# Mixture of experts in fp32: the experts' output is weighted, gated and added onto the residual in memory instead of in a combine stage

## The reference, cut to what matters

```python
h2 = rms_norm(x, norm2_w[l]) * (1 + sc2) + sh2
x = x + g2 * moe_ffn(h2, ...)
# in moe_ffn, for each expert e and its rows xe:
gu = xe @ w_gate_up[e] + b_gate_up[e]
gate, up = jnp.split(gu, 2, axis=-1)
gate = jnp.minimum(gate, SWIGLU_LIMIT)
up = jnp.clip(up, -SWIGLU_LIMIT, SWIGLU_LIMIT)
act = gate * jax.nn.sigmoid(SWIGLU_ALPHA * gate) * (up + 1)
yb = act @ w_down[e] + b_down[e]
# after all experts
y_rows = yb.reshape(n_rows, d) * row_w[:, None]
return jnp.zeros_like(hf).at[row_tok].add(y_rows)
```

## Time and profile before

| | |
|---|---|
| median of 3 runs | 2898.56 us (2898.47 to 2901.44) |
| the profiled execution's own time | 2901.38 us |
| its span | 2899.8 us |
| TensorE busy | 2509.1 us, 87% |
| VectorE busy | 1846.0 us, 64% |
| ScalarE busy | 1428.9 us, 49% |
| GpSimd busy | 483.5 us, 17% |
| DMA over the span | 572.65 MB, mean 197 GB/s |

### The profile page before, as it was taken

How to read it: one execution, slowest core, us unless ns; L and a number is a source line. 1 busy time by engine, 2 the same in 40 slices (tenths; PEclk the granted TensorE clock), 3 DMA queues, 4 the chain that set the end, 5 groups by cost and what they waited for, 6 DMA issues and landing times. The chain is left out here.

```text
span 2899.8 us, 39631 instructions
## 1 busy us (share of the span) xinstructions
PE 2509.1 (87%) x11553; PEld 1953.5 (67%) x11554; DVE 1846.0 (64%) x2784; ACT 1428.9 (49%) x2282; POOL 483.5 (17%) x504
## 2 busy tenths in 40 slices
PE   5899959898957999999988999999899999899930
PEld 2688835555845777777766777778667778677720
...
DMA packets 420768, 572.65 MB, mean 197 GB/s; under 512 B 20722, under 2 KB 319218, under 8 KB 419698
## 3 DMA queue, kind: packets, MB, share of 16 engines
...
HBM read 526.93 MB, written 45.12 MB: 197 GB/s over the span
## 5 line engine op out<-in xcount | busy, mean ns | idle before, releaser
L1550 ACT ACTIVATE d_whi<-d_raw 128x1024 fp32r<-128x1024 f32 x528 | 532.3, 1049 | 245.1 <-PE psum L1750 216.1
L1746 PE MATMUL psum<-d_whi,d_xthi 128*128 128x512 f32 x1536 | 616.9, 402 | 30.8 <-DVE d_xtlo L1622 23.3
L1631 DVE TENSOR_TENSOR d_wlo<-d_raw,d_whi 128x1024 fp32r<-128x1024 f32 x462 | 550.8, 1218 | 87.1 <-ACT d_whi L1550 85.7
L1746 PE MATMUL psum<-d_whi,d_xtlo 128*128 128x512 f32 x1536 | 604.8, 394 | 0.0
L1746 PE MATMUL psum<-d_wlo,d_xthi 128*128 128x512 f32 x1536 | 603.0, 393 | 0.0
L1631 DVE TENSOR_TENSOR d_wlo<-slab,d_whi 128x1024 fp32r<-128x1024 f32 x268 | 358.0, 1367 | 119.1 <-ACT d_whi L1550 119.1
L1550 ACT ACTIVATE d_whi<-slab 128x1024 fp32r<-128x1024 f32 x268 | 271.9, 1052 | 188.8 <-PE psum L1750 188.8
L1746 PEld LDWEIGHTS psum<-d_whi,d_xthi 128*128 128x128 f32 x1536 | 289.2, 188 | 108.0 <-issue 35.2
L1746 PE MATMUL psum<-d_whi,d_athi 128*128 128x512 f32 x768 | 310.6, 404 | 25.7 <-DVE d_atlo L1637 25.7
L1746 PEld LDWEIGHTS psum<-d_whi,d_xtlo 128*128 128x128 f32 x1536 | 289.0, 188 | 63.6
L1746 PEld LDWEIGHTS psum<-d_wlo,d_xthi 128*128 128x128 f32 x1536 | 289.6, 189 | 58.4
...
## 6 DMA issues: line engine op xcount, KB each, us to landing
...
d_raw<-in_w_down_dram SPq DMA_DIRECT2D x66, 2048.0 KB, 7.7
b_raw<-in_w_ada_dram SPq DMA_DIRECT2D x8, 2048.0 KB, 8.4
e_y<-y_d SPq DMA_DIRECT2D x8, 2048.0 KB, 13.6
...
a_xin<-in_x_dram ACTq DMA_DIRECT2D x2, 2048.0 KB, 9.3
```

What stands on the lines that cost most here:

```text
L1550: nc.scalar.activation(whi[j % 2][:, part, :], raw[j % NRAW][:, part, :], ACT.Copy).then_inc(whi_ok, 1)
L1631: nc.vector.tensor_tensor(wlo[j % 2][:, part, :], raw[j % NRAW][:, part, :], whi[j % 2][:, part, :].bitcast(F32), ALU.subtract).then_inc(w ...
L1746: nc.tensor.matmul(to, m_[b][:, k, :], w_[w][:, k, :], start=(k == 0 and q == 0), stop=False)
```

## The change

- `y_d` and `combine_block` are gone. `x1_d` becomes `acc_d`, with 128 rows of padding more. The experts' scatter writes there with `compute_op=ALU.add`, by token instead of by token and choice.
- `output` moves from ScalarE to VectorE and multiplies PSUM by the row's weight and by `gate2`. In slab 5 it stands after `xt_low` and before pieces 2 and 3.
- The row's weight comes from `topw_d`, a copy of `topw_all` in memory that SP stores at the end of the mixer stage. GpSimd gathers 128 of them for each block, one 4-byte element per row, when it has copied the destinations, and waits for them. For that the entries of the list have a third number, the index of the weight: one VectorE copy more per tile and choice. Padding has weight 0.
- GpSimd splits no weights any more; VectorE splits all four pieces of all slabs, and SP's loads and TensorE wait for VectorE alone.
- Before the first group GpSimd clears the padding of `acc_d` and `topw_d` and waits for that.
- After the last scatter SP copies the 4 MB of `acc_d` to `out` in one transfer.

The diff, cut to its core (declarations of semaphores, `c_entry`'s width, the new argument of `expert_block` and TensorE's simpler wait for `wlo` are left out; of `combine_block` only the removal of its head is shown):

```diff
...
     s.extk_d = dram("extk_d", [s.H, 4, s.T], F32)
-    s.x1_d = dram("x1_d", [s.T, s.D], F32)
+    s.acc_d = dram("acc_d", [s.T + P, s.D], F32)
+    s.topw_d = dram("topw_d", [s.T * s.TOPK + P, 1], F32)
...
-    s.list_d = dram("list_d", [s.E * s.T, 2], I32)
-    s.y_d = dram("y_d", [s.T * s.TOPK + P, s.D], F32)
+    s.list_d = dram("list_d", [s.E * s.T, 3], I32)
...
         chanmean = sb("a_chanmean", [P, P], F32)
-        nolist = sb("a_nolist", [P, s.E * T // P, 2], I32)
+        nolist = sb("a_nolist", [P, s.E * T // P, 3], I32)
...
                 own.link(nc.gpsimd.memset(chanmean[:, :], 1.0 / DC))
-                own.link(nc.gpsimd.memset(nolist[:, :, 0:1], 0))
-                own.link(nc.gpsimd.iota(nolist[:, :, 1:2].rearrange("p (a n) c -> p a (n c)", n=P),
-                                        pattern=[[0, s.E * T // P // P], [1, P]], base=s.TOPK * T, channel_multiplier=0))
+                own.link(nc.gpsimd.memset(nolist[:, :, :], 0))
+                for c, base in ((1, T), (2, s.TOPK * T)):
+                    own.link(nc.gpsimd.iota(nolist[:, :, c:c + 1].rearrange("p (a n) c -> p a (n c)", n=P),
+                                            pattern=[[0, s.E * T // P // P], [1, P]], base=base,
+                                            channel_multiplier=0))
...
                                  ).then_inc(slab_in, 16)
+                sp.wait_ge(topw_ok, 1)
+                sp.dma_start(s.topw_d[0:T * K4, :].rearrange("(t p r) a -> p t (r a)", p=P, r=K4),
+                             s.topw_all[:, :, :]).then_inc(topw_st, 16)
+                sp.wait_ge(topw_st, 16)
...
                     act.wait_ge(x1_ok, i + 1)
-                    act.dma_start(s.x1_d[bass.ds(i * P, P), :], xt[b][:, :]).then_inc(x1_st[b], 16)
+                    act.dma_start(s.acc_d[bass.ds(i * P, P), :], xt[b][:, :]).then_inc(x1_st[b], 16)
...
                         nc.vector.tensor_copy(entry[b][r][:, 0:1], tokf[:, bass.ds(i, 1)])
-                        ins = nc.vector.tensor_scalar(entry[b][r][:, 1:2], tokf[:, bass.ds(i, 1)], float(K4), float(r),
+                        nc.vector.tensor_copy(entry[b][r][:, 1:2], tokf[:, bass.ds(i, 1)])
+                        ins = nc.vector.tensor_scalar(entry[b][r][:, 2:3], tokf[:, bass.ds(i, 1)], float(K4), float(r),
...
                                                  .broadcast_to([P, NT, K4]), ALU.mult))
+                dve.sem_inc(topw_ok, 1)
...
         xg = [sb(f"d_xg{b}", [P, D], F32) for b in range(2)]
-        entry = [sb(f"d_entry{b}", [P, 2], I32) for b in range(2)]
+        entry = [sb(f"d_entry{b}", [P, 3], I32) for b in range(2)]
+        roww = [sb(f"d_roww{b}", [P, 1], F32) for b in range(2)]
+        roww_in, pad_st, added, out_st = ([sem(f"d_roww_in{b}") for b in range(2)], sem("d_pad_st"),
+                                          sem("d_added"), sem("d_out_st"))
...
-        POOL_SLABS, HALF = (2,), NP // 2
-        own_pieces = [HALF if j in POOL_SLABS else NP for j in range(SLABS)]
-        PER_DVE, PER_POOL = sum(own_pieces), HALF * len(POOL_SLABS)
...
-            return PER_DVE * (g + 1) + sum(own_pieces[:j]) + pieces
-        def split_by_pool(g, j, pieces):
-            return PER_POOL * (g + 1) + HALF * POOL_SLABS.index(j) + pieces
+            return NP * (SLABS * (g + 1) + j) + pieces
...
                     gb, jb = (g, j - NRAW) if j >= NRAW else (g - 1, j - NRAW + SLABS)
-                    sp.wait_ge(wlo_ok, split_by_dve(gb, jb, own_pieces[jb]))
-                    if jb in POOL_SLABS:
-                        sp.wait_ge(wlp_ok, split_by_pool(gb, jb, HALF))
+                    sp.wait_ge(wlo_ok, split_by_dve(gb, jb, NP))
...
-                sp.sem_inc(wlo_ok, PER_DVE)
-                sp.sem_inc(wlp_ok, PER_POOL)
+                sp.sem_inc(wlo_ok, NP * SLABS)
...
                 load(0, total(sp), 0)
+                sp.wait_ge(added, 1)
+                sp.dma_start(out[0, :, :], s.acc_d[0:T, :]).then_inc(out_st, 16)
+                sp.wait_ge(out_st, 16)
...
                 for b in range(2):
-                    own.link(nc.gpsimd.iota(ydst[b][:, :], pattern=[[0, 1]], base=s.TOPK * T, channel_multiplier=1))
+                    own.link(nc.gpsimd.iota(ydst[b][:, :], pattern=[[0, 1]], base=T, channel_multiplier=1))
...
                 own.link(nc.gpsimd.memset(two[:, :], 0))
+                pool.dma_start(s.acc_d[T:T + P, :], yst[0][:, :]).then_inc(pad_st, 16)
+                pool.dma_start(s.topw_d[T * s.TOPK:, :], yst[0][:, 0:1]).then_inc(pad_st, 16)
+                pool.wait_ge(pad_st, 32)
...
                     def scatter(b):
-                        pool.indirect_dma_start(out=s.y_d[:, :],
+                        pool.indirect_dma_start(out=s.acc_d[:, :],
                                                 out_offset=bass.IndirectOffsetOnAxis(ap=ydst[b][:, :], axis=0),
-                                                in_=yst[b][:, :], in_offset=None).then_inc(y_st[b], 16)
+                                                in_=yst[b][:, :], in_offset=None, compute_op=ALU.add
+                                                ).then_inc(y_st[b], 16)
...
                         s.settle(pool)
+                        pool.indirect_dma_start(out=roww[b][:, :], out_offset=None, in_=s.topw_d[:, :],
+                                                in_offset=bass.IndirectOffsetOnAxis(ap=entry[b][:, 2:3], axis=0)
+                                                ).then_inc(roww_in[b], 16)
...
                         pool.wait_ge(xg_in[b], 16 * (g + 1))
+                        pool.wait_ge(roww_in[b], 16 * (g + 1))
...
                         s.settle(pool)
-                    for j in POOL_SLABS:
-                        for q in range(HALF, NP):
-                            part = slice(PIECE * q, PIECE * (q + 1))
-                            pool.wait_ge(whi_ok, NP * (SLABS * g + j) + q + 1)
-                            nc.gpsimd.tensor_tensor(wlo[j % 2][:, part, :], raw[j % NRAW][:, part, :],
-                                                    whi[j % 2][:, part, :].bitcast(F32), ALU.subtract).then_inc(wlp_ok, 1)
...
                 s.settle(pool)
+                pool.sem_inc(added, 1)
...
-                def output(g, jd, b, sh):
-                    act.wait_ge(dn_mm, CRED + 2 * DN * g + 2 * jd + (b + 1) * sh)
-                    act.wait_ge(y_st[b], 16 * (g + 1))
-                    nc.scalar.activation(yst[b][:, jd * SL:(jd + 1) * SL], psum[:, 2 * ((GU + jd) % 2) + b, :],
-                                         ACT.Copy).then_inc(y_ok, sh)
...
                                 turned(g, j - 1, b, sh)
-                            elif j > GU:
-                                output(g, j - 1 - GU, b, sh)
                         split(g, j + 1, [3] if j < GU else [2, 3])
-                    for b in range(blocks):
-                        output(g, DN - 1, b, sh)
...
+                def output(g, jd, b, sh):
+                    dve.wait_ge(dn_mm, CRED + 2 * DN * g + 2 * jd + (b + 1) * sh)
+                    dve.wait_ge(y_st[b], 16 * (g + 1))
+                    dve.wait_ge(roww_in[b], 16 * (g + 1))
+                    cols = slice(jd * SL, (jd + 1) * SL)
+                    nc.vector.scalar_tensor_tensor(yst[b][:, cols], psum[:, 2 * ((GU + jd) % 2) + b, :],
+                                                   roww[b][:, 0:1], s.gate2[:, cols], ALU.mult,
+                                                   ALU.mult).then_inc(y_ok, sh)
...
                                 turned(g, j - 1, b, sh)
+                            elif j > GU:
+                                output(g, j - 1 - GU, b, sh)
                         split(g, j + 1, [3] if j < GU else [2, 3])
+                    for b in range(blocks):
+                        output(g, DN - 1, b, sh)
...
-def combine_block(nc, s, a, out):
...
-        s.release(nc)
-        combine_block(nc, s, arrays, out)
...
```

71 lines of the change are left out of this document (6 added, 65 removed).

## The result

The changed kernel takes **2849.49 us** (median of 4 runs, 2844.66 to 2853.01), the kernel before 2900.0 us beside it (2898.47 to 2903.51): a ratio of 0.9823, 95% interval 0.9804 to 0.9842. So 50.5 us are gained where I forecast 106.6, and the time lies 4.5 us above the range's upper end of 2845. The sign was right, the size was not.

A forecast was written before the change was run, and what follows sets the result against it. Bounds: TensorE in two-block groups, VectorE pacing one-block groups, a serial combine at the end. Tail -90.8, loop -21.1, head and mixer +5.3 make -106.6 on 2901.4; set against the runs' median, 2792 us, range 2768 to 2845.

The forecast's parts named there:

- Tail: From the last scatter's start to the end: 26.2 us instead of 117.0, so 90.8 us less.
- D: Time the addition in memory adds to a scatter's landing: taken as 2 us, between 0 and 6.1.
- My estimate of 23.4 us: Final copy, if reads and writes both count against 358 GB/s; 17 us was taken, this would end some 6 us later.
- Head and mixer: Before the first group: padding clearing 4.3 us, casts 1, top-weights store nothing; together 5.3 us more.
- Two-block groups: Expert loop: TensorE's waits for xtlo go as outputs leave ScalarE, 10.7 us less in 6 groups, 5.8 in 8.
- One-block groups, VectorE: Expert loop: stalls beside GpSimd's split go, two pieces and two outputs come; 1.2 us less per group.
- the ring: Loop dependency through scatter, row weights, entry, gather and transposes: period 41.1 to 41.7 us plus D, 43.4 with D = 2.
- 41.7 if nothing else binds: One-block group's time in us by VectorE's work alone, instead of 42.9.
- One-block groups, GpSimd's chain: Scatter to row gather grows 6.8 us plus D, using up 8.0 of slack; 10 groups lose 0.5 us each.
- 1.1 us of slack: One-block groups: ScalarE begins to need the gathered rows 1.1 us after TensorE, counted within 8.0 us of slack.
- a lead of 3 us: After a two-block group the scatter leaves about 3 us earlier relative to TensorE's end, so 8 groups keep 1.2 us gain.
- rival (b): The scatter's addition is dear, D about 5, slowing one-block groups and the tail: 2833 us; chance 24%.

The follow-up runs named there:

- this part alone: The kernel before with VectorE splitting every weight piece and GpSimd none, nothing else changed: 2882.66 us, ratio 0.9939.
- tiles last: The changed kernel with the next group's row weights gathered one step earlier, ahead of the scatter, its two new buffers declared last: 2757.46 us, ratio 0.9518.

## Why the prediction missed

**Tail: right.** -93.8 us for -90.8; D 2.2 for 2; the copy 14.9 for 17. My estimate of 23.4 us took the 358 GB/s per core of the Trainium skill (HBM Reference, Specifications) as one bound on reads and writes together. It is not: 4.19 MB read and as many written in 14.9 us are 563 GB/s. On the accumulating DMA (the Trainium skill, DMA: Bandwidth & Descriptors, Rules for kernel authors) the longer landing agrees with a destination that is read first, though the read bytes of the profile do not show it (below).

**Head and mixer: the sum right, by luck.** +4.8 for +5.3. The clearing of the padding was priced at 4.3 us (3 to 7). It costs 8.5: from GpSimd's last write to `d_two` to its first entry load are 11.3 us in after and 2.8 in before, and 10.9 to 11.3 against 2.8 in the experiments with and without the clearing. Against it stands a shorter way from the mixer stage to the experts' stage, for which the sum had no term. GpSimd's first instruction there, before and after:

```profile
867.52 2.65 POOL L1456 MEMSET d_braw<- 64x3072 f32 x1 [9.95 <-POOLq L55]
863.99 2.65 POOL L1462 MEMSET d_braw<- 64x3072 f32 x1 [5.01 <-POOLq L55]
```

Why the wait at the barrier is 4.9 us shorter, no run shows. The 1.2 us that are left of the 4.8 are near the 1 forecast for the mixer.

**Two-block groups: right in the mechanism, a little small.** The waits for `xtlo` are gone. Per 2 to 2 group 1.78 were forecast and 2.69 measured. 2.0 come with the outputs' move and 0.7 with the place of the tiles, a term that my sum did not have.

**One-block groups, VectorE: right.** The stalls of 3.43 and 1.31 us in the earlier trace rows are gone; 42.1 us forecast for this part alone, 41.92 measured. With outputs on VectorE and the weights off the ring a 1 to 1 group takes 41.82, where "41.7 if nothing else binds" stood.

**One-block groups, GpSimd's chain: this step failed.** I had seen the ring and said that it would bind, at 43.4 us in 10 groups. It binds at 47.05 and in all 18. Three parts of the term:
- From scatter to row gather I had 18.9 us growing by 6.8 - 2.0 (the later output lies elsewhere in the ring) + D = 25.7. In the 1 to 1 groups, for which 43.4 was forecast, it is 28.9 (mean of ten; 18.8 in before). Term by term the growth is: the scatter's landing 1.8 us where D was 2; the copies with the issues of the two gathers 3.5 for 2.4; the weights' landing and the loop registers, less the split, 3.2 for 2.4; and the way from the entry load to the row gather, which I had at nothing, 1.5 (6.1 us for 4.6). Durations of small transfers had been carried over from a place in the group where they are shorter. The rows then land in 6.5 us for 7.2.
- I counted 1.1 us of slack because ScalarE begins that much later. It is there only while TensorE's clock holds. With the rows in time the scatter follows their turning by 11.82 us (tiles last; 9.81 in before, and the 2.0 between them are the later outputs). Where the rows come late and the eight transposes take 1.1 to 1.3 us, it follows by 10.9 to 11.1, in 7 of the 18 groups. In the other 11 the clock is low after the pause, the transposes take up to 1.97 us (1.8 once), and the scatter mostly follows by 11.75: in the two lines shown above, 10.88 for the first and 11.74 for the second. The mean is 11.5 where I had 10.7.
- For the groups behind a two-block one I counted on a lead of 3 us. With the ring out of the way it is 2.3: TensorE turns the rows 32.3 us behind the first scatter in them and 30.0 in the others (tiles last), and they take 44.0 us, not 42.2. In after the rows are in only at 35.9, since the store of such a group has two scatters, the second 2.0 us behind the first, and it has to land as well: the copies begin 10.5 us after the first scatter, 7.5 in before. So the lead softened the ring without covering it: 3.7 us lost each instead of 1.2 gained, 39 us of the miss. The 1 to 1 groups, 4.0 instead of 0.5, are 35 us of it.

Against that stand 17 us that the two-block groups gained beyond the forecast, part of them only the later scatter of the group ahead (read as pairs, a one-block and a two-block group behind each other miss by 3.5 us, 28 us in all, and the 2 to 2 groups gain 5.5), and 1 us of the first group. In sum 56 us: 35.0 against -21.1.

The chances: my rival (b) had the right place and the wrong reason. It made the addition dear, D = 5, and gave 2833. D was as forecast, and a plain scatter wins only 22 us. The row weights' gathers, which are the smallest transfers of the change, cost, where they stand, the 92 us between after and the run that gathers them ahead with its tiles last. I had priced them in the ring, but left no width for the price: all slack was used up in my own count, so that each us of error was worth 10 to 18 us, and the range carried only D.
